# Two transformer blocks on one core: the last eviction of a run placed behind the next run's first weight split

## The reference

```python
# block 1
h = modulate(rmsnorm(x, norm1_g), sh1, sc1)
qa, ka, va, qkb, vb, ob, ib, fb, ga, gb = split(h @ w_in)
y = sigmoid(ga) * (attention(qa, ka, va) @ w_branch_a) + sigmoid(gb) * (mlstm(conv(qkb), vb, ...) @ w_branch_b)
x = x + gt1 * (y @ w_out)
x = x + gt2 * peer_ffn(modulate(rmsnorm(x, norm2_g), sh2, sc2))   # 16384 experts
# block 2, on rmsnorm(x, final_g)
fq, fk, fv, ff, sq, sk, sv, mq, gl = split(rmsnorm(x) @ w_in_2)
mk, mv = split(rmsnorm(mem) @ w_mem_kv)
gates = sigmoid(gl + b_gate)
merged = gates0 * (fox @ w_fox_o) + gates1 * (swa @ w_swa_o) + gates2 * (mem_att @ w_mem_o)
x = x + merged @ w_out_2;  x = x + peer_ffn_2(rmsnorm(x))
```

## Time and profile before

| what | value |
|---|---|
| median of three runs | 2507.2 us |
| the profiled execution | 2504.88 us |
| its span, first to last instruction | 2503.0 us |
| mean granted TensorE clock | 0.983 of full |
| busy share TensorE, VectorE, ScalarE, GpSimd | 93%, 69%, 51%, 9% |
| DMA, mean over the span | 156 GB/s |

### The profile page before, as it was taken

One profiled execution on the slowest core, in us unless ns is written; L12 is line 12 of the kernel. 1 busy time (PEld: TensorE's weight loads), 2 busy tenths in 40 slices (PEclk: granted clock), 3 DMA queues, 4 the chain that ended last, 5 costly groups with the idle time before them and its releaser, 6 DMA issues.

```text
span 2503.0 us, 48385 instructions
## 1 busy us (share of the span) xinstructions
PE 2316.3 (93%) x15404; PEld 2108.7 (84%) x15404; DVE 1726.1 (69%) x3636; ACT 1287.3 (51%) x2846; POOL 226.3 (9%) x285
## 2 busy tenths in 40 slices
PE   5998999999995699999899999999999976999998
PEld 4895899999995688888788858999999975788887
DVE  7575656888868866666544466548888869666665
ACT  3453345554547755555444563355545557555554
POOL 0000000000008800000000000000000049200000
PEclk8998999999999999999999999999999999999999
DMA  9751354555550156666335403445555520465664
GB/s 369 255 194 34 118 186 153 185 183 183 184 182 4 38 192 193 193 193 193 122 123 164 134 1 118 135 144 186 182 181 184 183 81 0 134 193 193 193 193 151
DMA packets 106072, 389.63 MB, mean 156 GB/s; under 512 B 12032, under 2 KB 12160, under 8 KB 105232
## 3 DMA queue, kind: packets, MB, share of 16 engines
q1 hardware_dynamic: 104688, 381.73, 47.1%
q10 hardware_dynamic: 992, 4.88, 0.5%
q0 software_dynamic: 320, 2.13, 0.2%
HBM read 387.64 MB, written 1.05 MB: 155 GB/s over the span
## 4 chain that ended last, share of the span: by engine, by line
PE 83%; POOL 8%; DVE 4%; ACT 2%; DMA 1%; issue 1%; SPq 0%; POOLq 0%; DVEq 0%; ACTq 0%
PE ps L571 19%; PE ps L538 16%; PE ps L533 16%; PE ps L535 16%; PE ps L575 9%; POOL scores L423 8%; DMA big<-ada_in 1%; DVE act_lo L1236 1%; PE ps L527 1%; PE ps L651 1%; PE ps L631 1%; DVE big L1243 1%; PE ps L683 1%; DVE act_hi L1235 1%; PE ps L671 0%
## 5 line engine op out<-in xcount | busy, mean ns | idle before, releaser
L892 ACT ACTIVATE hi<-raw 128x512 fp32r<-128x512 f32 x1356 | 775.5, 619 | 81.1 <-PE ps L538 79.3
L1161 DVE TENSOR_TENSOR lo<-raw,hi 128x512 fp32r<-128x512 f32 x844 | 546.0, 688 | 173.0 <-ACT hi L892 172.2
L533 PE MATMUL ps<-act_hi,hi 128*128 128x256 f32 x3376 | 546.5, 284 | 24.8 <-ACT hi L892 17.6
L538 PE MATMUL ps<-act_hi,lo 128*128 128x256 f32 x3376 | 545.4, 284 | 11.1 <-DVE lo L1161 11.1
L535 PE MATMUL ps<-act_lo,hi 128*128 128x256 f32 x3376 | 544.3, 284 | 0.0
L533 PEld LDWEIGHTS ps<-act_hi,hi 128*128 128x128 f32 x3376 | 467.5, 193 | 30.9 <-issue 14.7
L538 PEld LDWEIGHTS ps<-act_hi,lo 128*128 128x128 f32 x3376 | 467.8, 193 | 12.5 <-DVE lo L1161 12.5
L535 PEld LDWEIGHTS ps<-act_lo,hi 128*128 128x128 f32 x3376 | 467.5, 193 | 0.0
L1431 DVE TENSOR_TENSOR lo<-raw,hi 128x512 fp32r<-128x512 f32 x512 | 330.0, 689 | 129.7 <-ACT hi L892 122.7
L917 ACT ACTIVATE big<-ps 128x256 f32 (+1 forms) x346 | 132.9, 384 | 546.1 <-PE ps L538 546.1
L571 PE MATMUL ps<-hi,act_hi 128*128 128x512 f32 x1024 | 398.7, 389 | 0.0
(11 more groups left out here) (183 smaller groups left out, 1450.1 us busy)
## 6 DMA issues: line engine op xcount, KB each, us to landing
raw<-u SPq DMA_DIRECT2D x256, 512.0 KB, 3.6
raw<-v SPq DMA_DIRECT2D x256, 512.0 KB, 4.2
raw<-front SPq DMA_DIRECT2D x166, 512.0 KB, 3.6
big<-ada_in SPq DMA_DIRECT2D x48, 512.0 KB, 5.5
big<-biasA_in ACTq DMA_DIRECT2D x1, 2048.0 KB, 9.6
xT<-xT_in ACTq DMA_DIRECT2D x1, 1024.0 KB, 10.4
big<-keys_in ACTq DMA_DIRECT2D x1, 1024.0 KB, 12.9
scores<-memT_in POOLq DMA_DIRECT2D x1, 1024.0 KB, 5.2
```

What stands on the lines that cost most here:

```text
L533: pe.matmul(out_ap, hi_l(k), hi_r(k), start=(first and k == 0), stop=False, skip_group_check=True)
L538: mm = pe.matmul(out_ap, lo_l(k), hi_r(k), start=False, stop=(last and k == n - 1), skip_group_check=True)
L892: act.activation(hi[:, s, :, :], raw[:, rs, 4 * h:4 * h + 4, :], ACT.Copy).then_inc(hi_done, 1)
L1161: dve.tensor_tensor(lo[:, s, :, :], raw[:, rs, 4 * h:4 * h + 4, :], hi[:, s, :, :].bitcast(F32), ALU.subtract).then_inc(lo_done, 1)
```

## The change

Nine runs are named in `CHAINED`: va, qkb, vb, gates1, mv, fv, sk, sv, gates2. Ahead of these TensorE no longer waits for all outputs of the runs before; the wait of `outs_free` stays. On ScalarE the last eviction of the run ahead of each of them is handed over as `lead` and stands behind the split of both halves of the next run's first unit. The copy of va's values (ahead of vb) and the loads of the sigmoid table (ahead of gates1 and of gates2) move with it and stand behind that eviction. The load of the copy table ahead of fq_fk_sq_mq is taken out. SyncE's, VectorE's and GpSimd's programs are the same.

```diff
--- before.py
+++ after.py
@@ -64,6 +64,7 @@
     Run("swa_o", "K", 4), Run("mem_o", "K", 4), Run("wout2", "T", 8), Run("pq2", "T", 16),
     Run("u2", "U", 128), Run("v2", "O", 128),
 ]
+CHAINED = ("va", "qkb", "vb", "gates1", "mv", "fv", "sk", "sv", "gates2")
 RUNS = {}
 
 
@@ -587,7 +588,7 @@
                 r = RUNS[name]
                 if event is not None:
                     pe.wait_ge(act_ready, 2 * EV[event] + 1)
-                if r.kind != "O" and r.out0:
+                if r.kind != "O" and r.out0 and name not in CHAINED:
                     pe.wait_ge(taken, r.out0)
 
                 def body(g):
@@ -891,7 +892,7 @@
                     act.wait_ge(used, m - RING + 1)
                 act.activation(hi[:, s, :, :], raw[:, rs, 4 * h:4 * h + 4, :], ACT.Copy).then_inc(hi_done, 1)
 
-            def run(name, evict=None, peel=1):
+            def run(name, evict=None, peel=1, lead=None, defer=False):
 
                 r = RUNS[name]
 
@@ -899,6 +900,8 @@
                     for j in range(min(GROUP, r.units)):
                         for h in range(2):
                             weight_hi(r, g, j, h)
+                        if lead is not None and j == 0 and is_static(g) and g == 0:
+                            lead()
                         if evict and not (j == 0 and is_static(g) and g == 0):
                             out(g * GROUP + (j - 1), (r.out0 + j - 1) % 2)
 
@@ -910,8 +913,14 @@
                     body(0)
                 else:
                     groups(act, r, body, peel=peel)
+
+                def last_out():
+                    out(r.units - 1, (r.out0 + r.units - 1) % 2)
+
+                if defer:
+                    return last_out
                 if evict:
-                    out(r.units - 1, (r.out0 + r.units - 1) % 2)
+                    last_out()
 
             def to(dst, func=ACT.Copy):
                 return lambda u, p: act.activation(dst[:, bass.ds(u, 1), :].rearrange("p a t -> p (a t)"), p, func)
@@ -1041,15 +1050,23 @@
             act.dma_start(biasA, biasA_in).then_inc(bias_in_s, 16)
             act.dma_start(keysA, keys_in[0]).then_inc(keys_in_s[0], 16)
             act.preload_act_table(ACT.Copy)
-            run("ka_qa", lambda u, p: act.activation(kaqa[:, u, :], p, ACT.Copy, scale=1.0 if u < 4 else 64 ** -0.5),
-                peel=2)
-            run("va", to(vT1))
-            run("qkb", lambda u, p: act.activation(
-                upad[:, bass.ds(u, 1), 4:4 + T].rearrange("p a t -> p (a t)"), p, ACT.Copy))
-            copy_tokens("va")
-            run("vb", to(vT1))
-            act.preload_act_table(ACT.Sigmoid)
-            run("gates1", to(sig1, ACT.Sigmoid))
+            last_out = run("ka_qa", lambda u, p: act.activation(kaqa[:, u, :], p, ACT.Copy, scale=1.0 if u < 4 else 64 ** -0.5),
+                           peel=2, defer=True)
+            last_out = run("va", to(vT1), lead=last_out, defer=True)
+            last_out = run("qkb", lambda u, p: act.activation(
+                upad[:, bass.ds(u, 1), 4:4 + T].rearrange("p a t -> p (a t)"), p, ACT.Copy), lead=last_out, defer=True)
+
+            def lead_vb(last_out=last_out):
+                last_out()
+                copy_tokens("va")
+
+            last_out = run("vb", to(vT1), lead=lead_vb, defer=True)
+
+            def lead_gates1(last_out=last_out):
+                last_out()
+                act.preload_act_table(ACT.Sigmoid)
+
+            run("gates1", to(sig1, ACT.Sigmoid), lead=lead_gates1)
             copy_tokens("vb")
             log_gate(0, rows[0:4, 2, :])
             act.wait_ge(g_scan, 1)
@@ -1085,22 +1102,25 @@
             norm_squares("final", xT, (x_tile, 0))
             norm_rstd("mem")
             norm_rstd("final")
-            run("mk", to(mkT))
-            run("mv", to(values["mv"][0]))
+            last_out = run("mk", to(mkT), defer=True)
+            run("mv", to(values["mv"][0]), lead=last_out)
             copy_tokens("mv")
             act.wait_ge(x_ready, 3)
             act.wait_ge(act_ready, 2 * EV["mem"] + 2)
             norm_squares("norm1_2", xT)
             norm_rstd("norm1_2")
-            act.preload_act_table(ACT.Copy)
-            run("fq_fk_sq_mq", to(heads16))
-            run("fv", to(values["fv"][0]))
-            run("sk", to(skT))
-            run("sv", to(values["sv"][0]))
-            act.preload_act_table(ACT.Sigmoid)
+            last_out = run("fq_fk_sq_mq", to(heads16), defer=True)
+            last_out = run("fv", to(values["fv"][0]), lead=last_out, defer=True)
+            last_out = run("sk", to(skT), lead=last_out, defer=True)
+            last_out = run("sv", to(values["sv"][0]), lead=last_out, defer=True)
+
+            def lead_gates2(last_out=last_out):
+                last_out()
+                act.preload_act_table(ACT.Sigmoid)
+
             run("gates2", lambda u, p: act.activation(
                 sig2[:, bass.ds(u, 1), :].rearrange("p a t -> p (a t)"), p, ACT.Sigmoid,
-                bias=cols[:, bass.ds(COLS["b_gate"][0] + u, 1)]))
+                bias=cols[:, bass.ds(COLS["b_gate"][0] + u, 1)]), lead=lead_gates2)
             copy_tokens("fv")
             copy_tokens("sv")
             log_gate(1, rows2[0:8, 1, :])
```

## The result

The changed kernel takes 2493.73 us (median of four runs, 2490.89 to 2494.11); the kernel before, on the same chip, 2508.19 us (2506.87 to 2510.26). The ratio is 0.9939, 95% interval 0.9922 to 0.9956: 14.5 us less, where 13.9 were predicted and 2493.3 us.

A forecast was written before the change was run, and what follows sets the result against it. The prediction took the kernel as bound by TensorE, 93% busy, with time to win only where it stands still. Terms 6.55 + 5.48 + 1.86 = 13.9 us; 2507.2 - 13.9 = 2493.3 us, 8-in-10 range 2489.5 to 2498.5.

The forecast's parts named there:

- Five plain seams: va to qkb, mk to mv, fq_fk_sq_mq to fv, fv to sk, sk to sv: 1.31 us won at each, 6.55 us.
- the named wait alone: Lower case for the five plain seams: only the wait the timeline names (1.08 us) goes at each, 5.4 us.
- Two table seams: vb to gates1 and sv to gates2, where a table load stands: 2.74 us won at each, 5.48 us.
- The 0.23 us to spare: At the seams with a table load: second unit ready at t + 2.65 us, wanted by TensorE at t + 2.88.
- The first rival: Second unit late at both table-load seams, load holding the split 1.36 us longer: gain 11.6 us, time 2495.6; chance 0.08.
- qkb to vb: Seam with transposes and copies: TensorE goes straight from transposes into vb, 1.79 plus 0.07 for the first group, 1.86 us.
- The pause of 0.43 us: Idle time seen from ka_qa to va at a change of matmul kind; at vb it would cut the gain to 1.4 us.
- ka_qa to va: Seam covered by gate matmuls of 7.07 us; eviction and split take less than 3 us: nothing won or lost.
- the copy table's load: Load of 1.28 us on ScalarE ahead of fq_fk_sq_mq; ScalarE has seven microseconds to spare, so removal is worth zero.
- The second rival: VectorE and loads lose catch-up time at the seams; 6 us of 13.9 left, 2501 us, or within 0.2%; chance 0.06.
- The third rival: Shifted work puts more 1.2 GHz stretches, 3.4 us each, onto dense matmuls; six more make it slower; chance 0.03.

The follow-up runs named there:

- the order alone: The changed kernel with ScalarE's new order, but TensorE still waiting for all outputs ahead of every run: 2497.04 us, ratio 0.9949.
- the wait alone: The kernel before with only TensorE's wait for all outputs taken away at the nine runs, ScalarE's order as before: 2508.51 us, ratio 0.9999.
- the kernel with a second load: The changed kernel with one more table load behind the first at gates1 and two more at gates2: 2497.61 us, ratio 0.9957.
- block 1 alone: The kernel before with the change only at va, qkb, vb and gates1, block 2 as before: 2501.73 us, ratio 0.9974.
- the second profile: Profile of the changed kernel timed once more, unaltered: span 2490.6 us; measured 2492.48 us, ratio 0.9934 against the kernel before.

## Why the prediction was right

*What bounds the kernel.* Confirmed: time was won at the seams, where TensorE had stood still; what came and went elsewhere was the clock.

*The total.* Predicted 13.9, measured 14.5 by the medians, with an interval of some 11 to 19.6 us, and 14.04 by the starts of the matmuls at the seams. It is the second that confirms the sum; that the medians came so near is in part luck.

*Five plain seams, 6.55 us.* Measured 1.31 at each, 6.55. The lower end, the named wait alone, fell away: the slower first group behind a stop goes with the stop. That both parts of the change are needed was taken for granted in the prediction, and is shown by the order alone (0.59 of 1.31) and the wait alone (0).

*Two table seams, 5.48 us.* Measured 2 x 2.73. The 0.23 us to spare was the closest call of the sum, and the kernel with a second load confirms it to 0.02 us. The first rival, a late second unit, is refuted: the split follows 1.29 us behind the load's start (118.81 to 120.10), as in the row of before, and the Trainium skill's 2.66 us would have made it late. In gates2 the eviction of 0.47 us instead of 0.38 comes behind that split and changes nothing.

*qkb to vb, 1.86 us.* Measured 2.03, the one term that was mis-sized. The pause of 0.43 us that I feared from the earlier trace rows didn't come, and I had the two units' evictions 3.9 apart where they are 3.74. I added the transposes as 1.03 us, the time in which the last of them ends, but vb's first matmul starts 0.79 us after the first of them (105.82 to 106.61), 0.24 earlier than I reckoned. Against this, the first group behind them is still the slower one, 0.72 us, so the 0.07 that I counted as won is not.

*ka_qa to va, and the copy table's load: 0.* The first keeps its place behind the gate matmuls; the second was put back at no cost.

*The second rival* (VectorE or the loads lose their time to catch up): no wait for a load or for VectorE appeared from va to gates1, and block 1 alone won its whole 6.1.

*The third rival* (the clock): the mechanism is real and its size about right (a stretch of 3.4 us at 1.2 GHz cost 1.5 us each time that could be read off; at my rate of up to 3.4 us for 6.8 it would be up to 1.7), but the change isn't its cause. Such stretches come and go, and the changed kernel's profile has more of them than the one of before; the mean clock fell from 0.983 to 0.979, which I had named as its mark. Yet the kernel before has 0.978 to 0.983 from one execution to the next. I also wrote that the prediction is wrong if the waits go and the span doesn't fall by their sum. By the two first profiles that is what happened, 12.2 us of waits gone and the span 10.8 shorter; in the second profile it is 12.4 shorter. That sign was as poor as the mean clock, for the same reason. A mean clock of one profile against another is no mark of a change unless several executions of each are compared. For the same reason the prediction did well to give the time from the median and not from the profiled 2504.88: from there it would have been 2491.0.

## What to carry to other kernels

In a kernel bound by one engine, look at the seams between loops: work that a loop covers in its middle (the eviction of the last unit, a table load, copies) stands bare at its end, and its price is the distance of two evictions across the seam less their distance inside the loop. Put the next loop's first preparation ahead of that work, and take the consumer's blanket wait away as well: here the order alone gave two thirds, the wait alone nothing. Before the work is moved behind the first unit, count what it pushes back there: here 0.23 us were left of 2.88, and one more load would have cost 1.1 us.

## What the runs showed of the hardware

A table load holds ScalarE for 1.29 us in all, alone (118.81 to 120.10) or with three in a row (the last from 1344.78 to 1346.07), right behind an eviction from PSUM.

Whether TensorE's clock falls behind a stop differs from one execution to the next. Behind a stop of 2.50 us at one and the same place the granted clock fell to 1.2 GHz in six of eleven profiles and not in five, among them three of each with the same program up to there. Behind a stop of 2.2 and one of 2.51 us at a seam, the stretch at 1.2 GHz lasted 3.4 us and cost 1.5 us.

Among 31 executions of one kernel, in two series, each on one core of a chip of its own, the mean granted clock ran from 0.978 to 0.983 and the time from 2512.1 to 2506.1 us, about 1.3 us for each 0.001.
